# A hybrid decoder step on one core: two filler pieces, a group of sample scores and a weight split change places

## The reference

```python
h = rmsnorm(x); z = h @ w_in                      # ten 256-wide blocks and four 1024-wide gates
o_a = stick_breaking(q, k, v)                     # 4 heads: sigmoid scores, products of (1 - beta) from the right
o_b = hgrn2(...)                                  # gated linear recurrence in chunks, 4 heads in two halves
o_c = rg_lru(...); o_d = pool_mixer(...)
x += (sum_n sigmoid(gate_n) * (branch_n @ w_branch[n])) @ w_out
u = causal_dwconv(rmsnorm(x) @ w_up); x += (gelu(ua) * ub) @ w_down
x += sigmoid(rmsnorm(x) @ w_ple_gate) * (p @ w_ple)
```

## Time and profile before

| | |
|---|---|
| median of 3 runs | 1941.02 us (1940.99 to 1943.67) |
| profiled execution | 1940.31 us, span 1938.6 us, granted clock 0.989 |
| TensorE busy | 1866.9 us, 96% |
| VectorE busy | 1001.2 us, 52% |
| ScalarE busy | 568.4 us, 29% |
| GpSimd busy | 422.1 us, 22% |
| HBM traffic | 133 MB, 69 GB/s |
| chain that ended last | TensorE 89%, VectorE 4%, issue 3%, ScalarE 2% |

### The profile page before, as it was taken

The page is one execution under the profiler, slowest core; times in us unless marked ns, Lnnn a source line. Parts: engine busy times, 40 slices in busy tenths (PEclk is TensorE's granted clock), DMA queues, the critical chain, the costliest instruction groups (busy, mean ns, idle before and its releaser), DMA issues.

```text
span 1938.6 us, 28620 instructions
## 1 busy us (share of the span) xinstructions
PE 1866.9 (96%) x11857; PEld 1798.5 (93%) x11857; DVE 1001.2 (52%) x1170; ACT 568.4 (29%) x764; POOL 422.1 (22%) x213
## 2 busy tenths in 40 slices
PE   8999989799999999999999999999999999999998
PEld 5899888697678999999899999999999999999998
DVE  6922473643576121221434766866766766675522
ACT  4233423224465122111334311322221231133610
POOL 2323212112112122121211210211221122022231
PEclk9999999899999999999999999999999999999999
DMA  5211212114314221222321110110110111010121
GB/s 196 37 66 67 67 63 71 50 60 173 114 50 154 81 97 56 77 89 84 115 78 58 66 50 23 65 43 22 65 54 16 60 54 43 32 66 36 50 78 45
DMA packets 54295, 134.26 MB, mean 69 GB/s; under 512 B 12835, under 2 KB 28739, under 8 KB 51907
## 3 DMA queue, kind: packets, MB, share of 16 engines
q1 hardware_dynamic: 42114, 105.40, 15.8%
q0 software_dynamic: 5184, 19.01, 2.9%
q10 hardware_dynamic: 6912, 8.65, 1.3%
HBM read 110.82 MB, written 22.31 MB: 69 GB/s over the span
## 4 chain that ended last, share of the span: by engine, by line
PE 89%; DVE 4%; issue 3%; ACT 2%; SPq 1%; DMA 1%; POOL 0%; ACTq 0%; POOLq 0%; DVEq 0%
PE ps L703 59%; PE ps L1120 10%; PE ps L685 7%; PE pst L1120 3%; PE ps L848 2%; PE ps L666 2%; PE ps L769 1%; PE ps L927 1%; PE pst L948 1%; PE ps L961 1%; PE ps L672 1%; DVE Ml L2009 0%; DVE BIG L1868 0%; SPq L521 0%; DMA masks<-in_wb 0%
## 5 line engine op out<-in xcount | busy, mean ns | idle before, releaser
L2241 POOL TENSOR_TENSOR Ul<-BIG,Uh 128x1024 fp32r<-128x1024 f32 x60 | 145.2, 2419 | 710.4 <-ACT Uh L1559 630.6
L703 PE MATMUL ps<-Nh,Uh 128*128 128x352 f32 x1248 | 270.9, 325 | 4.3 <-issue 2.2
L703 PE MATMUL ps<-Nh,Ul 128*128 128x352 f32 x1248 | 269.5, 323 | 0.0
L703 PE MATMUL ps<-Fl,Uh 128*128 128x352 f32 x1248 | 269.3, 324 | 0.0
L703 PEld LDWEIGHTS ps<-Nh,Uh 128*128 128x128 f32 x1248 | 212.9, 189 | 5.8 <-issue 5.6
L703 PEld LDWEIGHTS ps<-Nh,Ul 128*128 128x128 f32 x1248 | 215.0, 188 | 0.0
L703 PE MATMUL ps<-Hh,Uh 128*128 128x352 f32 x936 | 203.6, 326 | 9.6 <-DVE Ml L2009 4.3
L703 PEld LDWEIGHTS ps<-Fl,Uh 128*128 128x128 f32 x1248 | 212.4, 188 | 0.0
L703 PE MATMUL ps<-Hh,Ul 128*128 128x352 f32 x936 | 202.1, 323 | 0.0
L703 PEld LDWEIGHTS ps<-Hh,Uh 128*128 128x128 f32 x936 | 159.4, 189 | 12.3 <-issue 5.0
L703 PEld LDWEIGHTS ps<-Hh,Ul 128*128 128x128 f32 x936 | 161.2, 188 | 0.0
(11 more groups left out here) (318 smaller groups left out, 3198.2 us busy)
## 6 DMA issues: line engine op xcount, KB each, us to landing
BIG<-in_wu SPq DMA_DIRECT2D x44, 512.0 KB, 3.6
H<-in_wd SPq DMA_DIRECT2D x11, 1024.0 KB, 4.8
BIG<-in_wgl SPq DMA_DIRECT2D x20, 512.0 KB, 4.3
BIG<-in_x SPq DMA_DIRECT2D x16, 528.0 KB, 6.3
gates<-BIG ACTq DMA_DIRECT2D x48, 176.0 KB, 1.9
BIG<-in_wz POOLq DMA_DIRECT2D x16, 512.0 KB, 3.8
BIG<-gates SPq DMA_DIRECT2D x12, 528.0 KB, 3.6
BIG<-in_wge POOLq DMA_DIRECT2D x12, 512.0 KB, 3.8
```

The costliest lines, as they stand in the source:

```text
L703: ins = nc.tensor.matmul(psb(3 * out + g), w[wp][:, k], x[xp][k][:, t0:t0 + n], start=(k == 0 and wp == xp), stop=(k == kk - 1 and wp == 1))
L2241: nc.gpsimd.tensor_tensor(Ul[:, half], uraw[:, half], Uh[:, half].bitcast(F32), ALU.subtract)\
```

## The change

- `start1` has 6 pieces instead of 4, `steps` 11 instead of 13. All pieces between keep their places, with numbers higher by two. ScalarE drains the new third and fourth of `start1` in the middle of its preparation.
- The attention's pieces stand at steps 0, 2, 6, 8, 10, 14, 16, 18, 20, 22, 24: the one at 12 goes to 10, those at 28 and 30 are gone.
- The second group of sample scores is at step 12 instead of 10, the scores of the new keys two pairs later.
- On GpSimd `tile_low(PLE, 0)` stands in the last FFN round ahead of the low part of the last down weights, instead of behind all three low parts.

```diff
-PLACES = (("states0", 2), ("levels0", 8), ("out0", 3), ("start1", 4), ("states1", 2), ("levels1", 8), ("out1", 2),
-          ("norms", 6), ("steps", 13))
-TWO_BANKS = 34
+PLACES = (("states0", 2), ("levels0", 8), ("out0", 3), ("start1", 6), ("states1", 2), ("levels1", 8), ("out1", 2),
+          ("norms", 6), ("steps", 11))
+TWO_BANKS = 36
-SCORES_AT = (4, 10)
-NEW_AFTER = 4
+SCORES_AT = (4, 12)
+NEW_AFTER = 6
-FILL_STEPS = {s: j for j, s in enumerate((0, 2, 6, 8, 12, 14, 16, 18, 20, 22, 24, 28, 30))}
+FILL_STEPS = {s: j for j, s in enumerate((0, 2, 6, 8, 10, 14, 16, 18, 20, 22, 24))}
@@ before(i), ScalarE
                 nc.scalar.activation(bd_, g, ACT.Sigmoid).then_inc(S("b_acts"), 1)
+                if i:
+                    gate_out(parts("start1")[2])
                 act.preload_act_table_set("natural_log_exp_and_others")
...
                 nc.scalar.activation(bdec[:, 8:16], b[:, SEQ + DL - 1:T:DL], ACT.Exp).then_inc(S("b_acts"), 1)
+                if i:
+                    gate_out(parts("start1")[3])
                 act.wait_ge(S("b_pre"), 7 * i + 5)
                 nc.scalar.activation(bE, bd_, ACT.Exp, scale=-1.0).then_inc(S("b_acts"), 1)
                 if i:
-                    for p in parts("start1")[2:]:
+                    for p in parts("start1")[4:]:
                         gate_out(p)
@@ w_round, GpSimd
                 pool.wait_ge(S("d_hi"), i + 1)
                 if last:
+                    tile_low(PLE, 0)
                     nc.gpsimd.tensor_tensor(Dl[:, :, 0:FIRST_D], draw[:, :, 0:FIRST_D],
                                             Dh[:, :, 0:FIRST_D].bitcast(F32), ALU.subtract).then_inc(S("d_lo"), 1)
@@ p_low, GpSimd
                 for q in range(2):
-                    tile_low(i + PLE, q)
+                    if q or not isinstance(i, int):
+                        tile_low(i + PLE, q)
```

## The result

The changed kernel took 1944.24 us (median of 12 runs, 1942.02 to 1947.02) where the kernel before took 1940.93 (median of 12 runs beside it, 1937.99 to 1943.67): a ratio of 1.0018, 95% interval 1.0010 to 1.0026. The profiled execution took 1944.3 us with a span of 1942.6, 4.0 us longer than before. The forecast was 1945.7 against the median, with a chance of 0.50 for slower by over 0.2% and of 0.41 for a change within it. The measured difference of 3.3 us lies just inside the 3.9 us that I had called indistinguishable, though the interval excludes no change at all. Lines behind ScalarE's edits carry numbers higher by 4 in the changed kernel (L1844 is L1848, L1559 is L1563), and by 5 behind GpSimd's (L2260 is L2265).

The account below looks back on a forecast made before the run. TensorE, busy 96% of the span, bounds the kernel, losing time only standing still or at its lower clock. Terms 2.8 + 0.9 - 6.1 - 2.5 + 9.6 = +4.7 gave 1945.7 us against the median; range 1939.5 to 1950.5.

Parts of the forecast that it names:

- the end: End of the FFN: the moved PLE low part delays GpSimd's queue and the last down product, +9.6 us (+9 to +12).
- the scores: Attention: the second sample scores at step 12 lose their wait for pages and slow clock, -6.1 us (-6.4 to -5).
- the slow clock of the turning: Second half's turning: idle time loses the clock again, 8.3 us from L817 to the state products' end (7.5 to 8.9).
- state products end: Second half's turning: state products end at 355.8, 2.8 us later than before (2.0 to 3.4).
- first level, on top: Behind the state products: GpSimd's split falls beside L1868's last two operations, +0.9 us (-1.9 to +1.5).
- late heads: Late attention heads: two pieces less bring pair 14's values forward, less a clock loss, -2.5 us (-3.8 to -1.5).
- clock behind it: Behind the last down product's start: slow clock after 11.5 idle microseconds, +0.3 us.
- ScalarE's delay: Second half's turning: of the third piece's drain, 0.86 us on ScalarE, some 0.35 us reach VectorE.
- the collision: Second half's turning: GpSimd's cast and subtraction get in between VectorE's eight L1844 operations, 3.1 us on top.
- The rival that only L1849 collides: Second half's turning: collision 0.9 us instead of 3.1 and the clock stays, total +0.3, 1941.3 us; chance 25%.
- the case to which I gave three chances in four: Late heads: 2.75 us idle ahead of pair 14's values loses the clock, costing 1.7 us, charged as 1.3.
- rival 2: End of the FFN: VectorE's sums take up the last down product's delay, that term 0, 1936.1 us; chance 7%.

Follow-up runs that it names:

- late_split: The changed kernel with the PLE low part back in its old place and GpSimd's split after piece 17 held behind VectorE's L1853: 1929.58 us, 0.9935.
- start_alone: The kernel before with only the two filler pieces moved from steps 28 and 30 to the second half's turning: 1940.45 us, 1.0000.
- warm_heads: late_split plus 12 products that nobody reads, in TensorE's idle time ahead of pair 14's values: 1927.72 us, 0.9932.
- tail_back: The changed kernel with the PLE low part back behind the three low parts of the last down product: 1935.45 us, 0.9965.
- tail_alone: The kernel before with only the PLE low part moved ahead in GpSimd's order: 1952.99 us, 1.0057.
- second_split: late_split with GpSimd's next split also held back, behind VectorE's third level: 1927.0 us, 0.9930.
- both_warm: second_split and warm_heads together: 1927.04 us, 0.9921.
- warm_levels: both_warm plus 28 products that nobody reads ahead of each half's first level: 1921.69 us, 0.9900.
- scores_alone: The kernel before with only the sample scores at step 12, the new keys' two pairs later and step 12's piece at step 10: 1936.28 us, 0.9967.

## Why the prediction was right

The direction and size came out: +4.0 us by the profiled executions for +4.7 (by the medians +3.3). The large terms, the end and the scores, are right in mechanism and size. The closeness of the sum is luck in part: the slow clock of the turning cost 1.1 us more than forecast, and 1.2 us that no term had came back before the attention. Term by term:

| step of the prediction | forecast | measured |
|---|---|---|
| L817 starts | 347.5 | 347.24 |
| state products end | 355.8 (+2.8) | 356.90 (+3.9) |
| first level, on top | +0.9 | +0.4 |
| given back up to attention's step 0 | 0 | -1.2 |
| scores two steps on | -6.1 | -5.9 |
| late heads | -2.5 | -2.4 |
| elsewhere in the attention | 0 | +0.1 |
| last down product against the front | +9.3 | +9.07 |
| clock behind it | +0.3 | 0 |
| sum | +4.7 | +4.0 |

The measured column compares the starts of the same instructions in the two profiled executions: L848 stands 4.4 us later, L989 3.1, L1051 5.1 earlier, the last down product's first matmul (1785.13 for 1781.11) and the first gate product (1812.10 for 1808.12) 4.0 later.

- **Turning.** ScalarE's delay was 0.31 us for 0.35 (336.39 against the earlier trace rows), the collision 2.9 us for 3.1. The rival that only L1849 collides is out: two of the eight L1848 stood, one for the cast and one for the subtraction, and late_split took the collision away by order alone. The Trainium skill (SBUF — State Buffer, "Who interferes with whom") has `tensor_scalar` among the operations that contend; the trace agrees, with 982 and 2439 ns for operations of 274. Its rule, that whoever issues first has the shared pair for the whole instruction, fits one instruction at a time: the eight are separate instructions, the second stood until the cast was over and the third until the subtraction was.
- **Too small: the slow clock after it.** I took 8.3 us from L817 to the end of the products, between 7.5 and 8.9; it was 9.66, outside that range. The clock was low from 0.7 us behind L817's start to 361.6, for 13.7 us and not for the 3.4 us near the end of the FFN. The upper bound was wrong as well: the 8.9 us of the kernel before were not all slow, since its clock was back at 351.4, 1.5 us ahead of the products' end (granted 0.76 over 350 to 353). The idle time was as forecast (2.94).
- **First level.** I placed the split beside L1868's last two operations, 8 us behind the products. The two pieces ran partly at the low clock, so it came 10.2 us behind them. Three things add up to the +0.4: the eight operations are 1.9 us shorter, with no split beside them; ScalarE's drain of the late second piece holds its activations back by 1.1 us; and the split costs 1.3 us at L1899 (1.98 us for 0.68). The collision was the right mechanism with the wrong victim, and the drain in ScalarE's queue was overlooked: the slow clock reached VectorE's chain through it.
- **Not foreseen: 1.2 us given back before the attention.** 0.45 us of it come at the first level itself, where the slow stretch lasted 3.4 us (371.8 to 375.3) and 6.8 before (365.1 to 371.9). The rest comes in the norms: the kernel before loses the clock at 470.9 to 474.3, the changed one at 460.6 to 464.0, where a wait of 0.97 us for ScalarE, which the kernel before has just behind this place, took up a part of the loss.
- **Scores.** -5.9 in the changed kernel, -5.6 alone. The charge of 0.3 for the next filler was 0.56 of waiting.
- **Late heads.** The last scores came 1.8 us earlier against the front, pair 14's values another 2.3 us, and the clock took 1.6 back: the case to which I gave three chances in four. start_alone shows the same -2.5, warm_heads the clock's share.
- **End.** The queue cost what its three durations add up to. The small VectorE operation fell from 2.44 us to 0.23, so ScalarE rounded the tile 1.6 us earlier against the front, as the prediction had it. tail_back and tail_alone both show the whole term, and rival 2 (the delay is caught up) is out: it needed the start of the last down product to move by less than 1 us against the front; it moved by 9.07, and the gate behind it by 9.0.

The parts alone give 1.0000, 0.9967 and 1.0057, together +0.24%, beside 0.18% measured: within their intervals they add.

## What to carry to other kernels

An instruction moved ahead in an in-order queue brings its wait along: look first at when what it waits for is done, then at who waits for those now behind it. Where VectorE is the chain that ends a wait, hold GpSimd's elementwise work off it by a semaphore, at that place and at the next one, because the work just shifts. And when an idle time of TensorE is filled or made, count the slow stretch behind it too: in this kernel the hole of 2.31 us ahead of pair 14's values cost 1.4 to 1.6 us in the matmuls behind it each time, and one of 2.23 us ahead of the last down product lost the clock in four profiled executions of nine.

## What the runs showed of the hardware

- The length of a slow stretch did not go by the idle time ahead of it: 13.7 us behind an idle time of 2.94 us ahead of L817, 3.4 us behind one of 4.95 (L848 in the changed kernel), 3.4 behind one of 2.31. TensorE was busy for 12.56 of 13 us of the longest. After 1.34 us ahead of the last scores the clock was lost in two executions (second_split, both_warm) and kept in six with the same wait.
- Products without use made the kernel faster: 56 of them ahead of the first levels cost no time, and the mean granted clock rose from 0.992 (both_warm) to 0.995 (warm_levels).
- An operation of VectorE that reads PSUM was not held up: in the kernel before, L1863 took 1.22 us at 357.23 beside GpSimd's cast (357.12 to 358.15), and as long in the first half with nothing beside it. In second_split four more that read PSUM (L1910) took 0.72 to 0.75 us each beside and behind the subtraction (372.02 to 374.40). L1887, which reads SBUF alone, took 3.20 us beside the split and 1.23 without it.
- Two of eleven profiled executions lost 2.4 us in the first half's turning behind an idle time of only 0.36 us (scores_alone, late_split), the others, with the same code there, nothing. Two spans are therefore first to be compared there.
